# Four bias tables made ahead of a neighbourhood attention, and two chunks of a norm rounded ahead of a row copy

## The reference, cut to what matters

```python
h = rms_norm(x, norm1) * (1 + sc1) + sh1          # shift, scale, gate: silu(cond) @ w_ada + b_ada
(na_q, na_k, na_v, pool_in, mla_cq, mla_ckv, mla_kpe, swa_q, swa_k, swa_v) = split(h @ w_in)
# mixer A: neighbourhood attention, 4 heads, grid of 8 rows x 64 columns, blocks of 16 query columns
s_loc = q @ k_local.T * scale + bias              # bias = rpb[:, dr, dc], a learned 2-D relative bias
s_loc = where(mask, s_loc, -1e30)
p = softmax(concat([s_loc, q @ ctx_k.T * scale])); o_na = p_local @ v_local + p_ctx @ ctx_v
# mixer B: mean over windows 2/4/8/16 minus the token, then a 64x64 matmul for each group
# mixer C: dense attention over a low-rank KV; mixer D: windowed attention with a sink
x = x + g1 * (concat(o_na, o_pool, o_mla, o_swa) @ w_out)
x = x + g2 * (relu(h2 @ mlp_w1)**2 @ mlp_w2)      # h2: the second modulated norm
```

## Time and profile before

| what | value |
|---|---|
| median of 3 runs | 1636.81 us (1631.8 to 1638.55) |
| the profiled execution's own time | 1636.24 us |
| its span, first to last instruction | 1634.1 us |
| PE / DVE / ACT / POOL busy | 1550.0 / 1099.7 / 845.6 / 116.1 us |
| mean granted clock of TensorE | 0.987 |
| scores of mixer A, layers 0 and 1 | from 262.17 and from 1060.78 us |
| first chunk-wise projection, layer 0 | from 36.41 us |

### The profile page before, as it was taken

The page is one execution under the profiler, slowest core; times in us unless marked ns, Lnnn a source line. Parts: engine busy times, 40 slices in busy tenths (PEclk is TensorE's granted clock), DMA queues, the critical chain, the costliest instruction groups (busy, mean ns, idle before and its releaser), DMA issues.

```text
span 1634.1 us, 30037 instructions
## 1 busy us (share of the span) xinstructions
PE 1550.0 (95%) x11642; PEld 1445.1 (88%) x11642; DVE 1099.7 (67%) x1951; ACT 845.6 (52%) x1483; POOL 116.1 (7%) x83
## 2 busy tenths in 40 slices
PE   5988998899999999999998889988999999999998
PEld 4865996699999999999976679956999999999998
DVE  4564446857788778787576433585868787878763
ACT  3666445765644444444355653466755454545442
POOL 1004003400000000000000220053000000000000
PEclk8999999999999999999999999999999999999999
DMA  9730443311222313222746123341303222222221
GB/s 327 245 104 1 77 140 107 104 53 52 78 88 68 104 57 99 72 84 79 248 139 196 39 25 115 107 132 50 98 33 104 73 83 78 78 78 79 78 78 65
DMA packets 150581, 160.00 MB, mean 98 GB/s; under 512 B 16358, under 2 KB 132776, under 8 KB 150440
## 3 DMA queue, kind: packets, MB, share of 16 engines
q1 hardware_dynamic: 149736, 157.87, 31.6%
q10 hardware_dynamic: 576, 0.16, 0.0%
q0 software_dynamic: 128, 0.05, 0.0%
HBM read 153.15 MB, written 4.65 MB: 97 GB/s over the span
## 4 chain that ended last, share of the span: by engine, by line
PE 80%; DVE 8%; ACT 7%; issue 2%; SPq 1%; DMA 1%; ACTq 0%; DVEq 0%
PE ps L1988 34%; PE ps L2393 20%; PE ps L2126 13%; PE ps L2409 4%; PE ps L2181 1%; DVE extrema L1640 1%; PE ps L2024 1%; PE ps L2203 1%; PE ps L1967 1%; ACT pt_c L898 1%; PE ps L2150 1%; SPq L730 1%; PE ps L2098 1%; DVE extrema L1623 1%; ACT w_hi L898 1%
## 5 line engine op out<-in xcount | busy, mean ns | idle before, releaser
L898 ACT ACTIVATE w_hi<-w_raw 128x512 fp32r<-128x512 f32 (+1 forms) x242 | 189.1, 781 | 193.0 <-PE ps L1988 100.0
L2393 PE MATMUL ps<-x_hi,w_hi 128*128 128x322 f32 x784 | 244.3, 312 | 0.6 <-DVE us L1815 0.6
L2393 PE MATMUL ps<-x_hi,w_lo 128*128 128x322 f32 x784 | 243.5, 311 | 0.0
L2393 PE MATMUL ps<-x_lo,w_hi 128*128 128x322 f32 x784 | 243.4, 310 | 0.0
L1988 PE MATMUL ps<-z_hi,w_hi 128*128 128x384 f32 (+1 forms) x1024 | 233.6, 309 | 0.0
L1988 PE MATMUL ps<-z_hi,w_lo 128*128 128x384 f32 (+1 forms) x1024 | 233.1, 309 | 0.0
L1988 PE MATMUL ps<-z_lo,w_hi 128*128 128x384 f32 (+1 forms) x1024 | 233.1, 309 | 0.0
L1340 DVE TENSOR_TENSOR w_lo<-w_raw,w_hi 128x512 fp32r<-128x512 f32 x212 | 146.8, 692 | 35.9 <-ACT w_hi L898 27.4
L2126 PE MATMUL ps<-w_hi,h_hi 128*128 128x256 f32 (+1 forms) x560 | 160.4, 286 | 2.7 <-ACT st L898 1.9
L2126 PE MATMUL ps<-w_hi,h_lo 128*128 128x256 f32 (+1 forms) x560 | 158.3, 283 | 0.0
L2126 PE MATMUL ps<-w_lo,h_hi 128*128 128x256 f32 (+1 forms) x560 | 158.2, 283 | 0.0
(11 more groups left out here) (292 smaller groups left out, 2876.2 us busy)
## 6 DMA issues: line engine op xcount, KB each, us to landing
w_raw<-in_mlp_w SPq DMA_DIRECT2D x64, 1024.0 KB, 5.4
ada_own<-in_w_ada SPq DMA_DIRECT2D x50, 512.0 KB, 4.5
w_raw<-in_w_in SPq DMA_DIRECT2D x14, 1024.0 KB, 7.7
ada_room<-in_w_ada SPq DMA_DIRECT2D x23, 512.0 KB, 9.0
ada_mix<-in_w_ada SPq DMA_DIRECT2D x17, 512.0 KB, 7.8
w_raw<-in_w_out SPq DMA_DIRECT2D x8, 768.0 KB, 5.3
ada_first<-in_w_ada SPq DMA_DIRECT2D x6, 512.0 KB, 9.1
x_in<-in_x_sample SPq DMA_DIRECT2D x1, 2048.0 KB, 8.5
```

Source lines behind the costliest of these rows:

```text
L898: do(nc.scalar.activation(out, in_, ACT.Copy), sem)
L2393: last = M.matmul(bank(b, XW), w[r][:, k, :], x_of(x, x_name)[:, k, :], start=k == 0 and q == 0 and not more, stop=k == 3 and q == 2, skip ...
```

## The change

Mixer A's tables get a place each: tables 0 and 1 as before, 2 and 3 in chunks 4 and 5 of `h_lo` and `h_hi`; the scratch tile `pool_d1` moves beside `pool_d0` to make room. GpSimd makes tables 1 and 2 once TensorE has finished the last projection, table 3 when the pooling mixer's second matmul is done, all ahead of its `normalise` loop. VectorE makes the low part of unit U+9 after the norm of `swkv`, ahead of table 0, and no longer in step 1 of the attention. In `first_norm` ScalarE rounds chunks 2 and 3 ahead of the ticks 15 to 19, that is, ahead of the copy of the fourth row; TensorE puts projections of single chunks between the last ticks.

```diff
-    pool_d = [at("pool_d0", H_HI + 4 * NTOK, [P, NTOK]), at("pool_d1", H_LO + 4 * NTOK, [P, NTOK])]
-    a_table = [at(f"a_table{i}", h + 6 * NTOK, [P, 4, 8, KCOLS]) for i, h in enumerate((H_LO, H_HI))]
+    pool_d = [at("pool_d0", H_HI + 4 * NTOK, [P, NTOK]), at("pool_d1", H_HI + 5 * NTOK, [P, NTOK])]
+    a_table = [at(f"a_table{i}", h + c * NTOK, [P, 4, 8, KCOLS])
+               for i, (h, c) in enumerate(((H_LO, 6), (H_HI, 6), (H_LO, 4), (H_HI, 4)))]
...
# GpSimd: in normalise
-                    if pair[0] == "A" and pair[1] in (None, 0, 1) and pair[2] == 1:
-                        b = 1 if pair[1] is None else pair[1] + 2
-                        if b == 1:
-                            pool.wait_ge(bias_scaled, l + 1)
-                        elif b > 1:
-                            pool.wait_ge(max_ready, signals(pair_at[(l, "A", b - 2, 1)]))
-                        build_table(do, pool, b, table_ready)
# GpSimd: ahead of normalise(l, "AD")
+                pool.wait_ge(bias_scaled, l + 1)
+                pool.wait_ge(p_done, proj_at[(l, "pool", NT - 1)] + 1)
+                build_table(do, pool, 1, table_ready)
+                build_table(do, pool, 2, table_ready)
+                pool.wait_ge(m_done, acc_ix.at[(l, "mix", 1)] + 1)
+                build_table(do, pool, 3, table_ready)
...
# ScalarE: first_norm
-                h_halves(2 * l, range(1, 2))
+                h_halves(2 * l, range(1, 4))
                 ada_ticks(48 * l, range(15, 20))
-                h_halves(2 * l, range(2, KC))
+                h_halves(2 * l, range(4, KC))
...
# VectorE: attention, and after norm(l, "swkv")
-                    if kind_list == "AD" and j == 1:
-                        split_lo(45 * l + 9)
+                split_lo(U + 9)
...
# TensorE: first_norm, layer 1 and layer 0
-                    ada_ticks(48 * l, range(7, 20))
-                    project_cq(l, 45 * l, range(KC))
+                    ada_ticks(48 * l, range(7, 16))
+                    project_cq(l, 45 * l, range(1))
+                    ada_ticks(48 * l, range(16, 19))
+                    project_cq(l, 45 * l, range(1, 2))
+                    ada_ticks(48 * l, range(19, 20))
+                    project_cq(l, 45 * l, range(2, KC))
...
-                    project_cq(0, 0, range(1))
-                    ada_ticks(0, range(15, 20))
-                    project_cq(0, 0, range(1, KC))
+                    project_cq(0, 0, range(2))
+                    ada_ticks(0, range(15, 19))
+                    project_cq(0, 0, range(2, 3))
+                    ada_ticks(0, range(19, 20))
+                    project_cq(0, 0, range(3, KC))
```

More of the change, by code:

```diff
@@ L677, in build_table @@
             mask = col_mask[:, {0: 0, 1: 1, 2: 1, 3: 2}[b], :].unsqueeze(1).unsqueeze(1)
-            do(eng.tensor_tensor(a_table[b % 2][:, :, :, :], bias, mask.broadcast_to([P, 4, 8, KCOLS]), ALU.add), sem)
+            do(eng.tensor_tensor(a_table[b][:, :, :, :], bias, mask.broadcast_to([P, 4, 8, KCOLS]), ALU.add), sem)
         block = ctx.enter_context(nc.Block())
@@ L1631, in maxima @@
                         v = s[:, :, 0:256]
-                        table = a_table[b % 2][:, 2 * hp:2 * hp + 2, :, :].rearrange("p h r c -> p h (r c)")
+                        table = a_table[b][:, 2 * hp:2 * hp + 2, :, :].rearrange("p h r c -> p h (r c)")
                         do(V.tensor_tensor(v, v, table, ALU.add))
```

## The result

The changed kernel takes 1623.86 us (median of 7 runs, 1620.78 to 1629.86) against 1635.01 us (7 runs of the kernel before, 1631.8 to 1638.55): a ratio of 0.993, 95% interval 0.9912 to 0.9948. The forecast was 1627.2 us. The profiled execution happens to be the slowest of the seven, 1629.86 us with a span of 1628.1 us and a mean granted clock of 0.985; the fastest, 1620.78 us, had 0.991.

The account below looks back on a forecast made before the run. TensorE, busy 1550.0 of 1634.1 us, was taken as the bound. Gains of 3.5 + 4.7 + 0.8 + 0.6 = 9.6 us turn 1636.24 into 1626.6, plus 0.6 for the median: 1627.2 us, own range 1624 to 1631, wider range 1621 to 1634.5.

Parts of the forecast that it names:

- The low part of U+9: VectorE operation of 2.29 us, moved into a 4.22 us wait ahead of table 0; to win 1.0 to 1.4 us.
- The tables ahead of A: GpSimd's tables 1 and 2, moved ahead of mixer A, may hold VectorE's table 0, at no cost given the cover.
- Table 3 and h_lo: Table 3 on GpSimd runs beside the second half of VectorE's h_lo; claimed to cost nothing.
- The rival that it is held: Table 3 holds VectorE's h_lo, 1.5 us in each layer, total 1630.2 us; chance 0.10.
- The three stretched operations: Tiny VectorE operations in mixer A beside GpSimd's tables; their 1.82, 1.11 and 0.49 us over 0.17 were to go.
- This remains, and VectorE has the room for it: Step 7's addition of b_ada, 1.38 us, still runs into a GpSimd multiplication; claimed that VectorE has room for it.
- The sum for A: Mixer A's stage, first score to D's first: 3.5 us sooner in layer 0, 4.7 in layer 1.
- The 0.7 us in each layer for the lower clock: Allowance in mixer A's stage for TensorE's granted clock falling again, about 0.7 us in each layer.
- What D takes back: Rival: mixer D, bound by VectorE, takes A's gain back, leaving the first norm's 1.4 us, 1635.4 us; chance 0.08.
- The first norm: ScalarE's chunks 2 and 3 rounded earlier, so chunk 4 starts sooner: 0.8 us in layer 0, 0.6 in layer 1.
- Slower: Rival: TensorE runs mixer A at the lower clock, 32 us against 9.6 won, about 1650 us; chance 0.04.
- closed up in part: Rival: another loop sets mixer A steps of 3.4 us, winning 1.5 to 2 us a layer, 1631.9 us; chance 0.15.

Follow-up runs that it names:

- e4: The changed kernel with the first norm's old order and the low part of U+9 back in attention step 1, so only the tables moved; 1629.63 us, ratio 0.9957.
- e2: The changed kernel with the first norm's old order, so the attention part alone; 1627.36 us, ratio 0.9946 to the kernel before.
- e6: The kernel before with mixer A's maximum written to PSUM and scaled from there, tables still in the loop; 1627.3 us, ratio 0.9945.
- e7: The changed kernel with VectorE's modulation tick ahead of the reciprocals in attention A and D; 1614.88 us, ratio 0.9868 to the kernel before.
- e10: The same kernel as e7, measured again; 1616.94 us, ratio 0.9874 to the kernel before.
- e1: The changed kernel measured again without an edit; 1626.8 us, ratio 0.994 to the kernel before.
- e3: The kernel before with only the first norm's new order; 1634.3 us, ratio 0.9983.
- e8: The changed kernel with ten more 512-column matmuls at the start of layer 1's first norm; 1627.92 us, ratio 0.9944 to the kernel before.
- e9: The kernel before with VectorE's modulation tick ahead of the reciprocals in attention A and D, no table moved; 1631.01 us, ratio 0.9957.
- e11: e7 with ten more 512-column matmuls in layer 1's first norm; 1619.3 us, ratio 0.9890 to the kernel before.

## Why the prediction was right, point by point

- **The low part of U+9.** Forecast inside the wait, with 1.93 us of cover left; 1.89 were left. It was to give 1.0 to 1.4 us from the score of pair 3 on; e4 against e2 shows 1.02 and 1.01.
- **The tables ahead of A.** Who is held came out the other way round. VectorE's table 0 started 0.07 us ahead of GpSimd's (250.21 and 250.28), and it was GpSimd that waited: 5.79 us for two tables that take 2.34 each, so 1.11 more. The prediction had VectorE held. By the Trainium skill ("SBUF — State Buffer", Who interferes with whom) whoever issues first keeps the shared pair for the whole instruction; the trace agrees, with the 1.11 us against the 1.15 that table 0 still had to run. It cost nothing, as there was cover either way: GpSimd's next work starts at 259.75.
- **Table 3 and h_lo.** The rival that it is held fell: 1.91 us for the two beside table 3 (259.75 to 262.09), unchanged. Its inputs are PSUM and one SBUF tile.
- **The three stretched operations.** Right, and e6 shows that the operand's place is most of what they cost in A: with the tables in the loop, and only the input in PSUM, A wins 2.6 and 3.7 us, where moving the tables alone wins 3.2 and 4.35 (e4).
- **"This remains, and VectorE has the room for it"**, on the addition of b_ada in step 7: the step that failed. It remained (1.37 us at 280.17), but there was no room: in e7 and e10 TensorE's step from pair 8 to pair 9 takes 3.05 us, against 3.46 in after and 3.60 in e1. That is half of the 0.9 us that e7 wins in stage A; most of the rest is the same addition in step 2 (0.52 us at 266.70). The prediction looked at step 7 alone. The same addition in step 17 (1.80 us in both layers already before) sets TensorE's longest wait in the stage. Asking of each stretched operation, over the whole stage, who waits behind it would have found it.
- **The sum for A.** 3.5 and 4.7 us forecast; 4.23 and 5.27 measured, the upper bounds (4.2 and 5.4) within 0.15 us. The walk over TensorE's own content was right. The 0.7 us in each layer for the lower clock was not paid in A: the granted clock is 1.00 in every window from 260 to 292.
- **What D takes back.** The prediction gave 0.08 to all of it. In layer 1 1.1 us of it were: stage D is 48.63 against 47.51, since the clock kept its level behind the 2.13 us wait before and fell after. That fall comes with the change and without: behind the same wait the score is slow in fourteen of 18 D stages, one of the two of before among them. So nothing here shows the change to be its cause. A gave 9.5 us, 1.3 more than forecast, and D took 1.3 back. A and D together give 4.04 and 4.15 us, 8.2 in all, which is by chance the 8.2 of the forecast.
- **The first norm.** The mis-sized term. Forecast 0.8 us in layer 0, with the row copy at 45.0 and chunk 4 at 48.0; they were at 43.52 and 46.51, so chunk 4 came 2.33 us sooner (2.77 in e3). I took 2.8 us for the second chunk's projection, near the 3.2 that its 15 matmuls take at the lower level (one in 0.21 us), and 2.3 for the four ticks. TensorE was back at the higher level from 39.12 us on, still inside the first chunk (its matmuls fall from 0.41 to 0.28 us there), and the second chunk took 1.8 us and the ticks 1.9. The windows of after:

```profile
36.00:40.00 4.00, 4.00 (x23) 4.00 (x24) 2.67 (x7) 3.80 (x7) 0.00 (x0) 0.62 1.11 328
40.00:44.00 4.00, 4.00 (x50) 2.94 (x50) 2.54 (x4) 1.76 (x3) 0.00 (x0) 1.00 0.35 92
```

  In the kernel before the same windows are granted 0.50 and 0.89. But the order alone, with the old timing of the clock left out of it, is worth 2.1 us: e2 (old order, 1.00 granted over 40 to 44) has chunk 4 at 48.15 and e1 at 46.01. In layer 1 chunk 4 stands 7.59 us behind the rounding that follows the third turned row (837.13 to 844.72, ScalarE), against 8.65 before (839.71 to 848.36): 1.1 us, its upper bound, against 0.6. A's first score in layer 0 came 1.57 us sooner, but "start" alone doesn't show the order's share: with the old order it is 258.03 to 264.30 us long, as the clock is at the lower level for 7 to 20 us in it. Where that is 17 us it is 262.17 with the old order (before) and 260.00 to 260.19 with the new one (e3, e8, e10), about 2.1 us. By the ratio of e3 the term is 2.8 us with an interval of 1.0 to 4.6, against 1.4.
- **Slower, or closed up in part**: nothing of either. Stage A has the length of the forecast, and the clock fell nowhere in it. The price of the slower case was added up wrongly: 32 us less the 9.6 won is 22 us over the kernel before, about 1659 us and not 1650.

The forecast gain of 9.6 us stands against 9.8 (e1, by its ratio) and 11.4 (first measurement, by its ratio). That they agree so closely is in part luck: the norm's term was half of what e3 gave, what D took back stood at nothing, and the profiles of the changed kernel lose 3.7 and 3.9 us in "between", a stretch of which the forecast said nothing beyond the norm's 0.6.

## What to carry to other kernels

SBUF-to-SBUF work on VectorE, even on 128x2 or 128x8 numbers, should not start behind a GpSimd operation that VectorE itself has just released: put it ahead of the release (0.9957 alone), or its input into PSUM (0.9945 alone, of which about half went with the clock). Each is an edit of a few lines. Of the 8.2 us that the change won in the stages A and D with all its moved tables, they won as much as 6.2 and 4.4, so try them first. And follow such a stretch to the engine that waits behind it, through the whole stage, since a fall of TensorE's clock can come on top of the longest wait. When two kernels are half a per cent apart, compare the stages that the edit touches, and the mean granted clock of the runs, before a median is put down to the edit.

## What the runs showed of the hardware

- A VectorE scaling of 128x2 numbers from SBUF to SBUF takes up to 1.99 us beside a GpSimd addition of 2.36 us (before); the same from PSUM to SBUF takes 0.16 us beside one of 2.34 or 2.36 (e6).
- GpSimd is held too: 1.11 us, by a VectorE operation of 1.22 us that began 0.07 us ahead of it (after).
- The clock fell behind the same wait of 2.13 us in fourteen D stages and not in four. Behind 0.47 to 0.49 us, in the eight D stages of e7, e9, e10 and e11, it stayed: the score takes 0.92 us in each, and the stages are 45.6 to 46.1 us long. Executions of the changed kernel spread from 1620.78 to 1629.86 us, the faster ones at the higher mean clock.
- With ten extra 512-column matmuls the granted clock was 1.00 where it had been 0.50 in the two profiles of the same kernel without them, and the time was no lower (0.9944 against 0.994, 0.9890 against 0.9874). Six other kernels had 1.00 there without them.
